# Last stage of a transformer layer: GpSimd issues the gathers of V rows in front of the lows of V and of the activations

## The reference

```python
hid = jnp.einsum('td,tkd->tk', xx, u[ee])            # per token: 128 picked experts
act = jax.nn.gelu(hid, approximate=False) * gg
out = jnp.einsum('tk,tkd->td', act, v[ee])           # 128 rows of V per token, weighted
```

## Time and profile before

| | |
|---|---|
| median of three runs | 3251.03 us |
| profiled execution, whole | 3249.3 us |
| its span | 3247.5 us |
| TensorE busy | 3145.8 us, 97% |
| VectorE busy | 2194.9 us, 68% |
| GpSimd busy | 1733.0 us, 53% |
| ScalarE busy | 1219.4 us, 38% |
| last stage, group 1 to the end | 2206.45 to 3247.5 us |

### The profile page before, as it was taken

One profiled execution on the slowest core, in us unless ns is written; L12 is line 12 of the kernel. 1 busy time (PEld: TensorE's weight loads), 2 busy tenths in 40 slices (PEclk: granted clock), 3 DMA queues, 4 the chain that ended last, 5 costly groups with the idle time before them and its releaser, 6 DMA issues.

```text
span 3247.5 us, 44094 instructions
## 1 busy us (share of the span) xinstructions
PE 3145.8 (97%) x17090; PEld 2847.3 (88%) x17090; DVE 2194.9 (68%) x3558; ACT 1219.4 (38%) x1899; POOL 1733.0 (53%) x843
## 2 busy tenths in 40 slices
PE   8999889899999999999999999998999999999997
PEld 6887878778899999999999999986888888888886
DVE  3513778544476778898989897755776666666665
ACT  4222557421122236566665656652222222121210
POOL 3420100112126666566666666747887878787773
PEclk9999999999999999999999999999999999999999
DMA  4364533321126666777777777897988787878783
GB/s 143 114 223 137 110 70 74 109 93 46 56 87 206 237 223 221 260 247 260 246 259 249 260 250 258 321 355 277 343 300 302 279 302 278 303 275 307 272 307 132
DMA packets 254403, 713.66 MB, mean 220 GB/s; under 512 B 21792, under 2 KB 79904, under 8 KB 247584
## 3 DMA queue, kind: packets, MB, share of 16 engines
q1 hardware_dynamic: 180512, 443.00, 40.2%
q0 software_dynamic: 73728, 268.47, 23.4%
HBM read 577.18 MB, written 134.22 MB: 219 GB/s over the span
## 4 chain that ended last, share of the span: by engine, by line
PE 71%; DMA 4%; POOL 3%; DVE 1%; issue 1%; ACT 1%; SPq 0%; DVEq 0%; POOLq 0%; ACTq 0%
PE banks L2304 29%; PE banks L1486 29%; PE banks L865 5%; PE banks L1499 5%; PE banks L844 2%; DMA score<-in_u,pick_u 2%; DMA v_raw<-in_v 1%; PE banks L873 1%; POOL side_lo L2180 1%; DVE score L1409 1%; POOL u_lo L1135 1%; DMA gate_in<-gate_d 0%; DMA u_raw<-in_uT 0%; POOL found L2152 0%; POOL w_lo L687 0%
## 5 line engine op out<-in xcount | busy, mean ns | idle before, releaser
L1135 POOL TENSOR_TENSOR u_lo<-u_raw,u_hi 128x1024 fp32r<-128x1024 f32 x127 | 370.7, 2919 | 390.5 <-ACT u_hi L1063 390.3
L1486 PE MATMUL banks<-side_hi,u_hi 128*128 128x384 f32 x2048 | 527.9, 338 | 0.0
L1486 PE MATMUL banks<-side_lo,u_hi 128*128 128x384 f32 x2048 | 519.7, 334 | 0.0
L1486 PE MATMUL banks<-side_hi,u_lo 128*128 128x384 f32 x2048 | 519.7, 334 | 0.0
L2304 PE MATMUL banks<-side_hi,act_hi 128*128 128x512 f32 x1488 | 459.4, 390 | 8.7 <-POOL act_lo L2184 6.6
L2304 PE MATMUL banks<-side_lo,act_hi 128*128 128x512 f32 x1488 | 458.9, 390 | 0.0
L2304 PE MATMUL banks<-side_hi,act_lo 128*128 128x512 f32 x1488 | 458.9, 390 | 0.0
L2209 DVE TENSOR_TENSOR acc<-acc,banks 128x1024 f32<-128x1024 f32 x192 | 234.2, 1220 | 323.5 <-PE banks L2304 307.3
L2123 ACT ACTIVATE side_hi<-v_raw 128x2048 fp32r<-128x2048 f32 x62 | 119.0, 1919 | 775.7 <-DMA v_raw<-in_v 608.3
L1486 PEld LDWEIGHTS banks<-side_lo,u_hi 128*128 128x128 f32 x2048 | 369.8, 188 | 0.0
L1486 PEld LDWEIGHTS banks<-side_hi,u_lo 128*128 128x128 f32 x2048 | 369.7, 188 | 0.0
(11 more groups left out here) (248 smaller groups left out, 5804.7 us busy)
## 6 DMA issues: line engine op xcount, KB each, us to landing
u_raw<-in_uT SPq DMA_DIRECT2D x128, 512.0 KB, 3.5
v_raw<-in_v SPq DMA_DIRECT2D x63, 1024.0 KB, 9.5
hid_d<-hid SPq DMA_DIRECT2D x128, 384.0 KB, 5.2
gate_d<-stage SPq DMA_DIRECT2D x48, 1024.0 KB, 8.1
act_in<-hid_d SPq DMA_DIRECT2D x63, 768.0 KB, 8.1
gate_in<-gate_d SPq DMA_DIRECT2D x31, 1536.0 KB, 15.0
w_raw<-in_w_in SPq DMA_DIRECT2D x5, 2048.0 KB, 9.3
k_hi<-k_hi_d SPq DMA_DIRECT2D x32, 256.0 KB, 8.0
```

The source lines that it names most:

```text
L1135: pool.tensor_tensor(u_lo[s % 2][:, :, :], u_raw[:, :, :], u_hi[s % 2][:, :, :].bitcast(F), ALU.subtract).then_inc(u_lo_ok, 1)
L1486: mm = pe.matmul(hid_ps[:, s % 2, half, 0:W], w[s % 2][:, ch], x[:, ch, GB * P + half * W:GB * P + (half + 1) * W], start=n == 0, stop=n = ...
```

## The change

GpSimd's order within a group. Before, the gathers of a place stand behind the low of that place; now they stand in front of it. The lows and the gathers keep their own orders, waits and sizes.

```diff
             for x in range(HALVES):
                 q = HALVES * g + x
+                gathers(g, 2 * x)
                 pool.wait_ge(v_hi_ok, q + HALVES + 1)
                 cols = slice(J * s + COLS * x, J * s + COLS * x + COLS)
                 pool.tensor_tensor(v_lo[:, cols], v_raw[:, :, :], v_hi[:, cols].bitcast(F),
                                    ALU.subtract).then_inc(v_lo_ok, 1)
-                gathers(g, 2 * x)
+                gathers(g, 2 * x + 1)
                 pool.wait_ge(a_hi_ok, q + HALVES + 1)
                 pool.tensor_tensor(a_lo[s][x], act_in[x][:, :, :], a_hi[s][x].bitcast(F),
                                    ALU.subtract).then_inc(a_lo_ok, 1)
-                gathers(g, 2 * x + 1)
         gather(PICKS - 1)
```

## The result

The changed kernel takes 3282.53 us (median of 4 runs, 3281.18 to 3286.59) where the kernel before takes 3250.52: ratio 1.0099, 95% interval 1.0084 to 1.0114. The forecast was 3278.5, slower. The span of the profiled execution grew by 3279.4 - 3247.5 = 31.9 us.

The account below looks back on a forecast made before the run. TensorE was taken to bound the kernel (71% of the span), so only its added waits count: 22.4 + 10 - 4.4 - 0.5 = 27.5 us on 3249.3 gives 3276.8, or 3278.5 us as a median; whole range 3262 to 3298.

Parts of the forecast that it names:

- its own signs of being wrong: Steady groups longer than 32.7 us, act_lo(3,1) starting before its pick, or stalls of groups 4 to 6 at 2 or 8 us.
- Part 1: Groups 3 to 6: act_lo(g,1) waits behind the fifth gather for a pick; TensorE stalls 6.8, 5.4, 4.8, 5.4, sum 22.4 us.
- The chain of 9.1 us: Groups 3 to 6, from the gates' start through pick and act_lo to TensorE: 1.68 + 3.75 + 3.51 + 0.15 us.
- part 3: Groups 4 to 6: gate load issued earlier in the group, its time to the gates unchanged; 4.4 us less stall.
- the floor of 2.3 us: Groups 4 to 6: gates cannot start before the fifth add, so 2.3 us of stall remain even with an instant load.
- rival (c): Stalls come but stay at 2.3 us, without the slow clock: +9 to +16 us; chance 0.07.
- Part 2: TensorE's clock falls to its lower level behind each of the four stalls: 4 x 2.5 = 10 us.
- Part 4: Groups 7 to 31: later lows cost nothing while act_lo(g,1) stays 2.6 to 3.4 us ahead of TensorE's need.
- Rival (b): Steady groups' margin fails, act_lo(g,1) late in each of 25 groups: +35 to +67 us in all; chance 0.12.
- Part 5: The start: act_lo(1,1) comes at the same time; gather 0's traffic delays the gate load 0 to 2 us, taken as 0.

## Why the prediction was right, and where it was not

The time was in the range and on the right side, 4 us from the median, and that nearness is luck. The forecast put 27.5 us into groups 3 to 6 and nothing into the later ones; the runs show 14.7 and 16.2 us. By its own steps it was half right; two errors of opposite sign met. Two of its own signs of being wrong came: steady groups took up to 34.56 us, where it allowed 32.7, and the stalls of groups 4 and 5 were 2.1 us, where it named 2.

**Part 1, right in mechanism.** Gather 11 stood in front of act_lo(3,1) and waited for pick 7, and the same in groups 4 to 6: TensorE waits on act_lo five times, once of them in group 1. The chain of 9.1 us measured 8.9. The sizes were wrong: stalls of 2.6, 2.1, 2.1 and 3.0 us, 9.9 in place of 22.4.

**The term that was mis-sized** is the gate load of part 3, "From issue to the gates I leave the time as it is". It took 11.3 us in group 2, at most 12.7 in group 3 (2304.47 to 2317.18, where the gates no longer waited for it) and 12.3 in group 5, in place of 13.9 and more. So the stalls fell to near the floor of 2.3 us which the bounds gave; rival (c) had these groups.

**Part 2, the clock**, forecast at 10 us. The changed kernel's granted clock was 0.95 in groups 3, 4 and 6 and 1.00 in group 5: three stretches of 3.4 us at 1.2 GHz, 1.7 us each, 5.1 in all. Stalls and clock make 15.0 of the 15.2 us that groups 3 to 6 lost (14.7 more than before, with the old 0.5).

**Part 4 failed.** It says "Cost: nothing", and followed GpSimd, V's load and TensorE's due time. Its conclusion for these held: act_lo(g,1) was never late in the steady groups, though only 1.6 to 3.4 us ahead, where it says 2.6 to 3.4. It left out SyncE: it asked who waits for a late low, and stopped at TensorE. That act_lo(g,0) ends at 15.6 us was in my own text. In the trace before, in the group that starts at 2610.23, it is through by the time the load of hidden values leaves, 12.9 us in, and the gates of the second half are through at 14.3 us; with 15.6 the first passes the second. From that point on SyncE's load of hidden values, and the gate load queued behind it, hang on GpSimd, and GpSimd hangs by the front gather on a pick behind the gates. A size was wrong there too: I took 2.3 us for the gather pair in front of act_lo(g,0), and it took 3.5 (2875.92 to 2879.46), because its first gather met VectorE's gates. The end came at 18.3 to 22.7 us and not at 15.6. Rival (b) had the right groups and the right order of size but the wrong mechanism: it looked for act_lo(g,1) to be late, and TensorE waited on adds.

**The rule of the Trainium skill**, SBUF — State Buffer, section on SBUF's two separate sides, on the shared ports: the gates took 4.65 us beside the pieces of side_lo, and 2.92 us (at 2874.47) in group 20 of the changed kernel, against 1.76 alone, so the trace still agrees that they disturb each other. But with SyncE's order turned they meet more and nothing is lost, so it was not the cause by itself. Nor was it nothing: the gather that such a product stretches is 1.3 us of the turn, and the turn is only 0.9 us too long. I had looked for the meeting at act_lo(g,1); it counted at a gather, which I had priced (2.29 us) in rival (b) alone.

**Part 5 held.** act_lo(1,1) ended 0.5 us later and group 2 began 0.35 us later, within the 0 to 2 us stated.

## What to carry to other kernels

When an instruction that waits is moved forward on one engine, follow each late result through every queue that waits for it, the DMA-issuing one too, until you are back at the wait: if the way closes, add up one turn and compare it with the bottleneck's period. A turn 1 us too long cost 16 us here, and swapping two issues took that back, so look at the margin of a loop and not only at the lateness of a single step. To see whether a loop binds, ask which distance stays fixed from group to group: in step with the bottleneck the mean turn equals its period in any case. And neither a transfer's time nor an issue's is a constant of the kernel: the same gate load took 11.3 us in one group and up to 16.4 in another of the changed kernel, and a gather 0.95 or 2.3 us by what VectorE was doing. That the other traffic sets the load's time is likely, but no run here held it fixed.

## What the runs showed of the hardware

An indirect DMA's issue on GpSimd (128 rows of 4 KB) took 0.93 to 0.96 us, and 1.3 to 2.5 us when it began while VectorE multiplied two operands from SBUF (the gates): it then ended 0.81 to 0.84 us behind that product, 440 times of 440 in 14 profiles. Two more began within 0.03 us of the product's start and weren't stretched.

How long TensorE's clock stays at the lower level differs. Behind gaps of 2.83 and 3.27 us between the starts of two matmuls (groups 3 and 6 of the changed kernel) it was 3.4 us, behind the gaps of 4.43 and 6.95 us of the kernel before 6.8 us. Of two gaps of 2.36 and 2.35 us (groups 4 and 5) the first was followed by the lower level and the second was not, and neither was one of 3.06 us in group 2. I had taken the longer stretch for all.

One GpSimd subtraction in more pieces is cheap: 128x2048 took 4.61 us whole and 5.04 in four pieces; 128x1536 took 3.5 us whole and 5.64 in sixteen, so 0.14 us for each further piece where no product of VectorE came between. The time of one 128x1024 subtraction elsewhere in the kernel before (2.68 us, L1177) had led me to expect 0.7 us.
